# Matrix-memory attention: the weight blocks of a head added on VectorE, and one product with ones per head in place of one per block

## The chip, the cores and the metric

One NeuronCore of one Trainium2 chip runs the whole program. The metric is the device time of one execution in microseconds (us). "Before" is given as the median of several runs; the profile is of one more execution, whose own time stands beside its span. Engines: PE is TensorE (its weight loads are listed as PEld), DVE is VectorE, ACT is ScalarE, POOL is GpSimd, SP issues the transfers of the weights.

## The reference, cut to what matters

The program is two transformer blocks over 512 tokens of width 1024. The change touches one stage of the second block, the matrix-memory (mLSTM) attention with 4 heads of width 128:

```python
def mlstm_chunkwise(q, k, v, i_pre, f_pre):      # computed chunk by chunk in the reference
    ...
    w_intra = jnp.exp(d_log - m_t[..., None])    # decay weights, causal
    s_qk = jnp.einsum('bhctd,bhcsd->bhcts', qc, kc) * w_intra
    num = jnp.einsum('bhcts,bhcse->bhcte', s_qk, vc) + ...
    den = jnp.sum(s_qk, axis=-1) + ...
    h = num / jnp.maximum(jnp.abs(den), jnp.exp(-m_t))[..., None]
...
    hm = mlstm_chunkwise(...)
    hm = rms_norm(hm, ml_norm.reshape(ML_HEADS, ML_HEAD_DIM))
    y_ml = jax.nn.sigmoid(o) * hm.reshape(bsz, s, ML_WIDTH)
```

For every query t, `num` is the decayed scores times the values, and `den` is the sum of the same decayed scores over all keys s up to t. Then the result is normalized and gated. The kernel computes the whole sequence of 512 queries at once, without the chunks: score times exp(difference of gates), masked to keys not after the query.

## The kernel before, in words

The five engines each have a queue in which the instructions stand in the order of the program text; engines wait for each other by semaphores. A signal such as `st_done(n)` means "the semaphore has counted n of these". A wait at the head of a queue holds everything behind it. The whole kernel is a list of stages, and each stage appends one function per engine. The matrix-memory stage is `s_mlstm`; after it comes `s_hyout`, the output projection.

In `s_mlstm` the work of a head `hd` (0 to 3) is cut into four units by blocks of 128 keys, `j` = 0 to 3. Unit `u = 4 * hd + j`. Because the mask is causal, unit j covers only the queries from 128 j on: 512, 384, 256 and 128 columns. Keys lie on the partitions, queries along the columns.

For each unit:

- TensorE, `scores(u)` (L2827): keys times queries into PSUM bank `u % 2`.
- ScalarE, `w(u)` (L2882): the decay weights into `msw`. GpSimd cuts the diagonal block of 128 columns to the causal mask (`affine_select`, L2973).
- VectorE (L2948): `mst` = `msw` times the scores in PSUM. It increments `st_done`.
- TensorE, `sums(u)`: first `mst` times the values into bank 4 + hd % 2 (L2838), then `mst` times a 128x128 matrix of ones into bank 6 + hd % 2 (L2840), both accumulated over the four units. The second gives `den` on all partitions.

For each head: `spread(hd)` (L2817, L2818) lays a row of the gates over all partitions for the weights; `finish(hd)` (L2847, L2848) does the same for the lower bound of the denominator; ScalarE's `magnitude(hd)` (L2887, L2888) squares `den` into `mden` and `num` into `msq`; VectorE's `larger(hd)` (L2927) takes the maximum of `mden` and the bound; TensorE's `squares(hd)` (L2854, L2856) sums squares over the width; ScalarE's `rms(hd)` takes Ln and Exp (L2894, L2897) into `mrb`; VectorE's `gain(hd)` (L2931, L2934) multiplies by it and by the output gate into `mnum`; ScalarE's `high` and VectorE's `low` split the result into `yh` and `yl` (L2901, L2938). `act_high` (L2786) and `dve_low` (L2790) do the same for the other half of the layer, within units 4 and 7.

The order of the queues is written out by hand. TensorE's, for each u: `scores(u + 2)`, which waits for `st_done(u + 1)`, that is for the `mst` product of unit u; then `sums(u)`; at j = 1 `spread(hd + 1)` and `squares(hd - 1)`; at j = 3 `finish(hd)`. VectorE's, for each u: the `mst` product; at j = 0 `larger(hd - 1)`; at j = 1 `low(hd - 2)`; at j = 3 `gain(hd - 1)`. ScalarE's, for each u: `w(u + 2)`; at j = 0 `magnitude(hd - 1)` and `high(hd - 2)`; at j = 2 `rms(hd - 1)`. Of the head 3, `magnitude`, `larger`, `rms` and `gain` come after the loop, and its `squares` (`last_squares`, L2980) stands inside the next stage.

GpSimd's queue goes on behind the last mask cut with splitting the weights of the next stage (`wlo`, L299, L300).

Of the kernel before, what the change touches and what calls it, by code (L numbers as in the profile page):

```python
# [18 lines left out]
ALU = mybir.AluOpType  # L19
AX = mybir.AxisListType.X  # L20

P = 128
# [71 lines left out]
def program(nc, d, out):  # L94
    with ExitStack() as ctx:
# [133 lines left out]
        mgt = at("mgt", X + 8192, [P, T])  # L229
        mnum = at("mnum", B + 82064, [P, 2, T])  # L230
        mden = at("mden", B + 86160, [P, T])

        prj = at("prj", B, [P, DT, T])

# [2558 lines left out]
        def s_mlstm(before):  # L2793
# [4 lines left out]
            def part(buffer, j, first=0, last=T):  # L2798
# [3 lines left out]
             ss_done, ln_done, rb_done, t_done, p_done, h_done, l_done) = local(  # L2802
                "st", s=16, m=4, w=16, st=16, cut=16, pv=16, nm=4, abs=4, mx=4, sq=4, ss=4, ln=4,
                rb=4, t=4, p=4, h=4, l=4)

            def pe(pe):

                def spread(hd):

                    if hd >= 2:  # L2810
                        pe.wait_ge(*mx_done(hd - 1))
                    if hd == 0:
                        pe.wait_ge(*scaled(20))
                        pe.wait_ge(*row_high(3))
                        pe.wait_ge(*row_low(2))
                    pick = selr[:, hd * P:(hd + 1) * P]
                    pe.matmul(PS3[:, 2 + hd % 2, :], pick, rowsr[:, 3, :], start=True, stop=False, skip_group_check=True)  # L2817
                    pe.matmul(PS3[:, 2 + hd % 2, :], pick, rowsr[:, 4, :], start=False, stop=True,  # L2818
                              skip_group_check=True).then_inc(m_done.s, 1)

                def scores(u):
                    hd, j = units[u]
                    if u >= 2:
                        pe.wait_ge(*st_done(u - 1))
                    elif u == 0:
                        pe.wait_ge(*key_scaled(1))
                    pe.matmul(PS3[:, u % 2, j * P:T], qkc[:, 4 + hd, j * P:(j + 1) * P], qkc[:, hd, j * P:T],  # L2827
                              start=True, stop=True, skip_group_check=True).then_inc(s_done.s, 1)

                def sums(u):  # L2830
                    hd, j = units[u]
                    pe.wait_ge(*st_done(u + 1))
                    if hd == 0:
                        pe.wait_ge(*v_kept(max(2, j + 1)))
                    if hd >= 2 and j == 0:
                        pe.wait_ge(*t_done(hd - 1))
                        pe.wait_ge(*ln_done(hd - 1))
                    pe.matmul(PS3[:, 4 + hd % 2, j * P:T], vml[:, j, hd * P:(hd + 1) * P], part(mst, j, j * P),  # L2838
                              start=j == 0, stop=j == 3, skip_group_check=True)
                    pe.matmul(PS3[:, 6 + hd % 2, j * P:T], c_("ones"), part(mst, j, j * P),  # L2840
                              start=j == 0, stop=j == 3, skip_group_check=True).then_inc(pv_done.s, 1)

                def finish(hd):

                    pe.wait_ge(*w_done(4 * hd + 4))
                    pick = selr[:, hd * P:(hd + 1) * P]
                    pe.matmul(PS3[:, 2 + hd % 2, :], pick, rowsr[:, 0, :], start=True, stop=False, skip_group_check=True)  # L2847
                    pe.matmul(PS3[:, 2 + hd % 2, :], pick, rowsr[:, 2, :], start=False, stop=True,  # L2848
                              skip_group_check=True).then_inc(nm_done.s, 1)

                def squares(hd):
                    pe.wait_ge(*sq_done(hd + 1))
                    pe.wait_ge(*mx_done(hd + 1))
                    pe.matmul(PS3[:, 6 + hd % 2, :], c_("ones"), msq[:, :], start=True, stop=False,  # L2854
                              skip_group_check=True)
                    pe.matmul(PS3[:, 6 + hd % 2, :], c_("ones"), mden[:, :], start=False, stop=True,  # L2856
                              skip_group_check=True).then_inc(ss_done.s, 1)
                spread(0)
                scores(0)
                scores(1)  # L2860
                pe_values(pe, 3)
                for u in range(16):
                    hd, j = units[u]
                    if u + 2 < 16:
                        scores(u + 2)
                    sums(u)
                    if j == 1 and hd < 3:
                        spread(hd + 1)
                    if j == 1 and hd >= 1:
                        squares(hd - 1)  # L2870
                    if j == 3:
                        finish(hd)

            def act(act):
                act.preload_act_table_set("natural_log_exp_and_others")

                def w(u):
                    hd, j = units[u]
                    act.wait_ge(*m_done(hd + 1))
                    if u >= 4:  # L2880
                        act.wait_ge(*st_done(u - 3))
                    act.activation(part(msw, j, j * P), PS3[:, 2 + hd % 2, j * P:T], ACT.Exp,  # L2882
                                   bias=ccol[:, j, hd:hd + 1], scale=-1.0).then_inc(w_done.s, 1)

                def magnitude(hd):
                    act.wait_ge(*pv_done(4 * hd + 4))
                    act.activation(mden[:, :], PS3[:, 6 + hd % 2, :], ACT.Square, scale=EPS ** 0.5).then_inc(abs_done.s, 1)  # L2887
                    act.activation(msq[:, :], PS3[:, 4 + hd % 2, :], ACT.Square).then_inc(sq_done.s, 1)  # L2888

                def rms(hd):  # L2890
                    act.wait_ge(*ss_done(hd + 1))
                    if hd >= 1:
                        act.wait_ge(*t_done(hd))
                    act.activation(mrb[:, :], PS3[:, 6 + hd % 2, :], ACT.Ln, bias=epsc[:, 4:5],  # L2894
                                   scale=1.0 / P).then_inc(ln_done.s, 1)
                    act.wait_ge(*ln_done(hd + 1))
                    act.activation(mrb[:, :], mrb[:, :], ACT.Exp, scale=-0.5).then_inc(rb_done.s, 1)  # L2897

                def high(hd):
                    act.wait_ge(*p_done(hd + 1))  # L2900
                    act.activation(yh[:, 4 + hd, :], mnum[:, hd % 2, :], ACT.Copy).then_inc(h_done.s, 1)  # L2901
                w(0)
                w(1)
                act_last_split(act)
                for u in range(16):
                    hd, j = units[u]
                    if u + 2 < 16:
                        w(u + 2)
                    if hd >= 1 and j == 0:
                        magnitude(hd - 1)  # L2910
                    if hd >= 2 and j == 0:
                        high(hd - 2)
                    if hd >= 1 and j == 2:
                        rms(hd - 1)
                    if u in rg_steps["act"]:
                        rg_steps["act"][u](act)
                magnitude(3)
                high(2)
                rms(3)
                high(3)  # L2920

            def dve(dve):
# [13 lines left out]
                def low(hd):  # L2936
                    dve.wait_ge(*h_done(hd + 1))
                    dve.tensor_tensor(yl[:, 4 + hd, :], mnum[:, hd % 2, :], yh[:, 4 + hd, :].bitcast(F32),  # L2938
                                      ALU.subtract).then_inc(l_done.s, 1)
                for u in range(16):  # L2940
                    hd, j = units[u]
                    if u == 0:
                        dve.wait_ge(*gated(1))
                    dve.wait_ge(*s_done(u + 1))
                    dve.wait_ge(*cut(u + 1))
                    if u >= 4:
                        dve.wait_ge(*pv_done(u - 3))
                    dve.tensor_tensor(part(mst, j, j * P), part(msw, j, j * P), PS3[:, u % 2, j * P:T],  # L2948
                                      ALU.mult).then_inc(st_done.s, 1)
                    if u == 0:  # L2950
                        dve_value(dve, 0)
                        dve_value(dve, 1)
                    elif u < 3:
                        dve_value(dve, u + 1)
                    if u in rg_steps["dve"]:
                        rg_steps["dve"][u](dve)
                    if hd >= 1 and j == 0:
                        larger(hd - 1)
                    if hd >= 2 and j == 1:
                        low(hd - 2)  # L2960
                    if hd >= 1 and j == 3:
                        gain(hd - 1)
# [780 lines left out]
```

## Time and profile before

| | |
|---|---|
| median of 3 runs | 2518.85 us (2516.84 to 2520.12) |
| the profiled execution, its own time | 2519.44 us |
| its span, first to last instruction | 2517.7 us |
| TensorE busy | 2488.9 us, 99% |
| VectorE busy | 1421.9 us, 56% |
| ScalarE busy | 1045.1 us, 42% |
| GpSimd busy | 972.7 us, 39% |
| mean granted TensorE clock | 0.997 |
| the matrix-memory stage on TensorE | about 1355.4 to 1398.9 us |

Busy time of an engine says how much it could be in the way, not that it is. The chain that ended last is followed back from the last instruction, at each step to what released it; its pieces add up to the span, so what stands in it is what the time is made of. In the chain a matrix product is shown by the time that it adds, in the time line by its own length, which overlaps the next one by some 0.16 us. A product of plain float32 operands is listed as two records; "x2" in a row is one product.

### The profile page before, as it was taken

The numbers are of one execution on the slowest core, as the hardware profiler recorded it, in microseconds if no ns is written. First come the engines' busy times: TensorE is split into PE (matmuls) and PEld (weight loads), VectorE is DVE, ScalarE is ACT, GpSimd is POOL, SyncE is SP. The second block draws the span as 40 slices with busy tenths as digits, with TensorE's granted clock in tenths as the row PEclk, the third lists the DMA queues.
The fourth block names the chain that finished last, engine by engine and source line by source line (L and its number), as shares of the span: only waits on it lengthen the run. The fifth ranks groups of instructions, "written<-read, shape, count | busy, mean of one in ns | idle before, by whom it ended". The sixth has DMA issues, their size and how long they took to land.

```text
span 2517.7 us, 37538 instructions
## 1 busy us (share of the span) xinstructions
PE 2488.9 (99%) x13732; PEld 2104.4 (84%) x13732; DVE 1421.9 (56%) x1894; ACT 1045.1 (42%) x1551; POOL 972.7 (39%) x721
## 2 busy tenths in 40 slices
PE   9999999999999989999999999999999999999999
PEld 8999999957777789988777788888887778888887
DVE  6988114376436688841595655553355855666213
ACT  5556224374343455542564332222244643222222
POOL 3001553303234400045353555555453045555443
PEclk9999999999999999999999999999999999999999
DMA  4333332202112222333321223232332122222322
GB/s 161 101 105 95 109 104 99 78 1 68 59 59 94 96 87 100 100 115 96 109 93 51 85 99 99 92 100 92 100 126 80 55 86 99 100 92 100 105 97 84
DMA packets 72187, 230.96 MB, mean 92 GB/s; under 512 B 9297, under 2 KB 9553, under 8 KB 72082
## 3 DMA queue, kind: packets, MB, share of 16 engines
q1 hardware_dynamic: 64128, 216.27, 26.2%
q10 hardware_dynamic: 7954, 13.26, 1.7%
q8 instruction: 69, 1.13, 0.2%
q14 instruction: 36, 0.29, 0.0%
HBM read 220.58 MB, written 5.24 MB: 90 GB/s over the span
## 4 chain that ended last, share of the span: by engine, by line
PE 63%; DVE 1%; ACT 0%; issue 0%; DVEq 0%; ACTq 0%
PE PS L305 17%; PE PS L307 17%; PE PS L306 17%; PE PS L811 2%; PE PS L812 2%; PE PS L813 2%; PE PS L3374 1%; PE PS L3391 1%; PE PS L3355 1%; PE PS L2827 0%; PE PS L2840 0%; PE PS L2838 0%; PE PS L3159 0%; PE PS L3362 0%; PE PS L2445 0%; PE PS L2444 0%
## 5 line engine op out<-in xcount | busy, mean ns | idle before, releaser
L299 POOL TENSOR_TENSOR wlo<-wraw,whi 128x512 fp32r<-128x512 f32 (+2 forms) x350 | 458.5, 1310 | 1481.3 <-ACT whi L291 1481.1
L305 PE MATMUL PS<-xh,whi 128*128 128x512 f32 (+1 forms) x1640 | 608.7, 371 | 3.9 <-POOL wlo L300 1.6
L307 PE MATMUL PS<-xh,wlo 128*128 128x512 f32 (+1 forms) x1640 | 601.7, 367 | 0.0
L306 PE MATMUL PS<-xl,whi 128*128 128x512 f32 (+1 forms) x1640 | 601.4, 367 | 0.0
L291 ACT ACTIVATE whi<-wraw 128x1024 fp32r<-128x1024 f32 (+2 forms) x350 | 350.2, 1001 | 594.0 <-PE PS L307 579.4
L300 POOL TENSOR_TENSOR wlo<-wraw,whi 128x512 fp32r<-128x512 f32 (+2 forms) x350 | 522.5, 1493 | 0.0
L305 PEld LDWEIGHTS PS<-xh,whi 128*128 128x128 f32 x1640 | 307.4, 187 | 59.6 <-POOL wlo L300 2.5
L307 PEld LDWEIGHTS PS<-xh,wlo 128*128 128x128 f32 x1640 | 307.5, 187 | 51.3
L306 PEld LDWEIGHTS PS<-xl,whi 128*128 128x128 f32 x1640 | 307.5, 187 | 51.1 <-issue 1.4
L305 PE MATMUL PS<-hid2h,whi 128*128 128x512 f32 x560 | 218.4, 390 | 0.0
L306 PE MATMUL PS<-hid2l,whi 128*128 128x512 f32 x560 | 217.9, 389 | 0.0
L307 PE MATMUL PS<-hid2h,wlo 128*128 128x512 f32 x560 | 217.9, 389 | 0.0
L1441 DVE TENSOR_TENSOR h<-PS,h 128x512 f32<-128x512 f32 x24 | 16.6, 690 | 204.9 <-PE PS L307 204.9
L1257 DVE TENSOR_TENSOR gp<-PS,rb_up 128x1024 f32<-128x1024 f32 x24 | 29.4, 1224 | 174.2 <-PE PS L307 174.2
L1544 DVE TENSOR_SCALAR f<-PS 128x528 f32<-128x528 f32 (+1 forms) x16 | 11.2, 699 | 203.9 <-ACT sq L1528 193.4
L305 PEld LDWEIGHTS PS<-hid2h,whi 128*128 128x128 f32 x560 | 105.1, 188 | 22.9 <-DVE h L1441 0.8
L306 PEld LDWEIGHTS PS<-hid2l,whi 128*128 128x128 f32 x560 | 105.1, 188 | 21.9 <-issue 0.2
L307 PEld LDWEIGHTS PS<-hid2h,wlo 128*128 128x128 f32 x560 | 105.1, 188 | 21.7
L493 ACT ACTIVATE xh<-h,vec 128x512 fp32r<-128x512 f32 (+1 forms) x64 | 45.9, 726 | 156.9 <-DVE h L1441 107.0
L1267 DVE SCALAR_TENSOR_TENSOR gc<-gp,vec,gc 128x512 f32<-128x512 f32 x96 | 111.0, 1213 | 0.0
L305 PE MATMUL PS<-hid1h,whi 128*128 128x264 f32 x352 | 100.3, 285 | 0.0
L306 PE MATMUL PS<-hid1l,whi 128*128 128x264 f32 x352 | 100.3, 285 | 0.0
(546 smaller groups left out, 5170.2 us busy)
## 6 DMA issues: line engine op xcount, KB each, us to landing
wraw<-w_up_dram SPq DMA_DIRECT2D x96, 512.0 KB, 3.2
wraw<-w_dn_dram SPq DMA_DIRECT2D x48, 512.0 KB, 3.2
wraw<-w_f1gu_dram SPq DMA_DIRECT2D x44, 512.0 KB, 3.2
wraw<-w_f2gu_dram SPq DMA_DIRECT2D x44, 512.0 KB, 3.2
wraw<-w_hyin_dram SPq DMA_DIRECT2D x24, 512.0 KB, 3.3
wraw<-w_win_dram SPq DMA_DIRECT2D x18, 512.0 KB, 3.3
wraw<-w_gate_dram SPq DMA_DIRECT2D x16, 512.0 KB, 3.2
wraw<-w_pg_dram SPq DMA_DIRECT2D x16, 512.0 KB, 3.3
```

The costliest lines, as they stand in the source:

```text
L291: act.activation(whi[:, s, 0:size], wraw[:, s, 0:size], ACT.Copy).then_inc(hi_done.s, 1)
L299: pool.tensor_tensor(wlo[:, s, 0:half], wraw[:, s, 0:half], whi[:, s, 0:half].bitcast(F32), ALU.subtract)
L300: pool.tensor_tensor(wlo[:, s, half:size], wraw[:, s, half:size], whi[:, s, half:size].bitcast(F32), ALU.subtract).then_inc(lo_done.s, 1)
L305: pe.matmul(out_, whi[:, s, a:b], xhi, start=start, stop=False, skip_group_check=True)
L306: pe.matmul(out_, whi[:, s, a:b], xlo, start=False, stop=False, skip_group_check=True)
L307: return pe.matmul(out_, wlo[:, s, a:b], xhi, start=False, stop=stop, skip_group_check=True)
L493: act.activation(dh[:, t, 0:n], h[:, t, 0:n], ACT.Copy, scale=v_(gain, t)).then_inc(high.s, 1)
L811: pe.matmul(o, oph[:, jj, a], high[:, kt, :], start=start and kt == 0, stop=False, skip_group_check=True)
L812: pe.matmul(o, oph[:, jj, a], low[:, kt, :], start=False, stop=False, skip_group_check=True)
L813: ins = pe.matmul(o, opl[:, jj, a], high[:, kt, :], start=False, stop=kt == 3, skip_group_check=True)
L1257: dve.tensor_tensor(gp[:, :, 2:T + 2], bank(0, 2), spread(rb_up, 1), ALU.mult).then_inc(g_read.s, 1)
L1267: ins = dve.scalar_tensor_tensor(gc[:, m, :], gp[:, m, tap:T + tap], vec[:, bass.ds(2 * j + (cw + FF2T * tap + m), 1)], gc[:, m, :], ALU.m ...
```

## The change

`sums(u)` no longer issues the product with ones. In its place VectorE adds the `mst` blocks of a head into a tile `macc` of 512 columns (two tiles, for even and odd heads): behind the `mst` product of each unit comes `add(u)`, at j = 0 a copy of the first 128 columns, and at j = 1, 2, 3 an add of the 384, 256 and 128 columns from 128 j on; at j = 1 the earlier part is read from the unit 0 block itself. TensorE issues one product of ones with the whole `macc` per head, `over_keys(hd)`, 512 columns: for heads 0 to 2 behind the sums of unit 4 hd + 4, for head 3 behind `finish(3)`, at the end of the stage. `magnitude(hd)` waits for it by a new signal.

```diff
+        macc = [at("macc0", B + 95568, [P, T]), at("macc1", B + 88208, [P, T])]
...
+            added, summed_over = local("su", add=16, over=4)
...
                     pe.matmul(PS3[:, 4 + hd % 2, j * P:T], vml[:, j, hd * P:(hd + 1) * P], part(mst, j, j * P),
-                              start=j == 0, stop=j == 3, skip_group_check=True)
-                    pe.matmul(PS3[:, 6 + hd % 2, j * P:T], c_("ones"), part(mst, j, j * P),
                               start=j == 0, stop=j == 3, skip_group_check=True).then_inc(pv_done.s, 1)
+
+                def over_keys(hd):
+                    pe.wait_ge(*added(4 * hd + 4))
+                    pe.matmul(PS3[:, 6 + hd % 2, :], c_("ones"), macc[hd % 2][:, :], start=True, stop=True,
+                              skip_group_check=True).then_inc(summed_over.s, 1)
...
                     if u + 2 < 16:
                         scores(u + 2)
                     sums(u)
+                    if j == 0 and hd >= 1:
+                        over_keys(hd - 1)
                     if j == 1 and hd < 3:
                         spread(hd + 1)
                     if j == 1 and hd >= 1:
                         squares(hd - 1)
                     if j == 3:
                         finish(hd)
+                over_keys(3)
...
                 def magnitude(hd):
                     act.wait_ge(*pv_done(4 * hd + 4))
+                    act.wait_ge(*summed_over(hd + 1))
                     act.activation(mden[:, :], PS3[:, 6 + hd % 2, :], ACT.Square, scale=EPS ** 0.5).then_inc(abs_done.s, 1)
...
+                def add(u):
+                    hd, j = units[u]
+                    over = macc[hd % 2]
+                    dve.wait_ge(*st_done(u + 1))
+                    if j == 0:
+                        if hd >= 2:
+                            dve.wait_ge(*summed_over(hd - 1))
+                        dve.tensor_copy(over[:, 0:P], part(mst, 0, 0, P)).then_inc(added.s, 1)
+                    else:
+                        dve.wait_ge(*added(u))
+                        so_far = part(mst, 0, P) if j == 1 else over[:, j * P:T]
+                        dve.tensor_tensor(over[:, j * P:T], so_far, part(mst, j, j * P), ALU.add).then_inc(added.s, 1)
...
                     dve.tensor_tensor(part(mst, j, j * P), part(msw, j, j * P), PS3[:, u % 2, j * P:T],
                                       ALU.mult).then_inc(st_done.s, 1)
+                    add(u)
```

## Rows read from the trace of the kernel before

**Rows 1.** The page: busy time of the engines, and the chain that ended last.
```profile
PE 2488.9 (99%) x13732; PEld 2104.4 (84%) x13732; DVE 1421.9 (56%) x1894; ACT 1045.1 (42%) x1551; POOL 972.7 (39%) x721
...
PE 63%; DVE 1%; ACT 0%; issue 0%; DVEq 0%; ACTq 0%
```

**Rows 2.** The chain, in order of time: start, length, engine and line.
```profile
1372.79 0.86 PE PS L2840 x2
...
1374.52 0.65 PE PS L2840 x2
...
1375.82 1.05 PE PS L2854 x2
1376.88 0.86 PE PS L2856 x2
...
1379.02 0.43 PE PS L2840 x2
...
1380.32 0.24 PE PS L2840 x2
1380.56 0.68 DVE mst L2948
1381.28 0.70 PE PS L2827 x2
...
1385.64 0.23 PE PS L2818
```

**Rows 3.** The time line of VectorE: start, length, line, tiles, idle before and releaser.
```profile
1374.67 2.29 DVE L2790 TENSOR_TENSOR yl<-grg,yh 128x2048 fp32r<-128x2048 f32 x1
1379.15 0.75 DVE L2931 SCALAR_TENSOR_TENSOR mgt<-PS,vec,mrb 128x512 f32<-128x512 f32 x1 [2.19 <-ACT mrb L2897]
...
1381.28 0.69 DVE L2927 TENSOR_TENSOR mden<-mden,PS 128x512 f32<-128x512 f32 x1
1381.89 0.55 DVE L2948 TENSOR_TENSOR mst<-msw,PS 128x384 f32<-128x384 f32 x1
1382.35 0.68 DVE L2938 TENSOR_TENSOR yl<-mnum,yh 128x512 fp32r<-128x512 f32 x1
```

**Rows 4.** The time line of ScalarE, the same columns.
```profile
1371.66 1.92 ACT L2786 ACTIVATE yh<-grg 128x2048 fp32r<-128x2048 f32 x1
...
1377.77 0.69 ACT L2894 ACTIVATE mrb<-PS,epsc 128x512 f32<-128x512 f32 x1 [1.23 <-PE PS L2856]
1378.49 0.63 ACT L2897 ACTIVATE mrb<-mrb 128x512 f32<-128x512 f32 x1
...
1380.58 0.60 ACT L2887 ACTIVATE mden<-PS 128x512 f32<-128x512 f32 x1 [0.63 <-PE PS L2840]
```

**Rows 5.** The list of TensorE's waits: us in total, times, longest us.
```profile
PEld PS L1822 <- DVE spf L1877: 9.4, 12, 1.7
...
PEld PS L2827 <- DVE mst L2948: 1.3, 3, 0.5
```

**Rows 6.** The time line of TensorE, the same columns as rows 3.
```profile
1380.82 0.39 PE L2848 MATMUL PS<-rowsr,selr 4*128 4x512 f32 x1
1381.28 0.70 PE L2827 MATMUL PS<-qkc 128*128 128x256 f32 x2
```

**Rows 7.** Groups by shape, 1355.38 to 1398.88: count, then busy us, mean ns.
```profile
L2948 DVE TENSOR_TENSOR mst<-msw,PS 128x128 f32<-128x128 f32 x4 | 1.1, 284 | 2.6 <-PE PS L2827 2.6
```

**Rows 8.** Time lines of VectorE and GpSimd at the start of the next stage.
```profile
1400.63 1.00 DVE L2938 TENSOR_TENSOR yl<-mnum,yh 128x512 fp32r<-128x512 f32 x1
```
```profile
1399.35 1.74 POOL L300 TENSOR_TENSOR wlo<-wraw,whi 128x512 fp32r<-128x512 f32 x1
```

**Rows 9.** Three windows: us, busy PE PEld DVE ACT POOL, granted clock, DMA share, GB/s.
```profile
903.00:907.00 4.00, 0.00 (x0) 0.00 (x0) 2.39 (x3) 3.99 (x5) 0.00 (x0) 0.61 0.00 0
907.00:911.00 4.00, 3.98 (x19) 3.98 (x20) 4.00 (x5) 1.43 (x2) 0.00 (x0) 0.54 0.44 136
500.00:510.00 10.00, 8.92 (x54) 6.05 (x53) 7.17 (x9) 8.43 (x11) 0.00 (x0) 1.00 0.00 0
```

## The prediction

> **What bounds the kernel now.** I read the page first. [rows 1] TensorE is busy for 99% of the span, no other engine for more than 56%, and the chain that ended last runs through TensorE almost alone. So 1 us taken off TensorE's queue is 1 us of time, as long as TensorE does not start to wait for something; and every us that it is made to wait counts in full. Next I read the stage that the change touches, by the chain of waits in order of time over one head (hd = 1) [rows 2]. The reader is to see a solid row of TensorE pieces with one other link: VectorE's `mst` product at 1380.56. Then the same head on VectorE and ScalarE [rows 3, 4]: both have holes, so their work costs nothing unless it stands between two TensorE pieces. Last the list of waits [rows 5]: in these four heads TensorE's score product waits for VectorE 3 times, 1.3 us in all. All times in us.
>
> I call the units 0 to 15 u, with hd = u // 4 and j = u % 4; "sums" is the product with the values (L2838) and "ones" the product with ones behind it (L2840).
>
> **What TensorE no longer does.** Each product shows as two records, and the chain gives the pair. Ones cost 0.86 at j = 0, 0.65 at j = 1, 0.43 at j = 2 and 0.24 at j = 3, where I count 0.22 (a quarter of the 0.86) and leave the rest to the step to `finish` [rows 2]. That is 2.16 a head, 4 x 2.16 = 8.64 in all.
>
> **What it does instead.** One full-width product a head, the shape of the 0.86: 4 x 0.86 = 3.44. For hd = 0 to 2 it stands behind sums of the next head's j = 0, among products of its own kind. The fourth comes behind `finish(3)`, where the operand type changes: after such a change the same shape took 1.05 and not 0.86 [rows 2], so 0.19 more. TensorE's own work: -8.64 + 3.44 + 0.19 = **-5.0**.
>
> **What it has to wait for now.** This decides. Before, the last ones of head 0 came at the end of unit 3, and ScalarE's `magnitude` (the squares into `mden` and `msq`) ran while TensorE did `finish` and the scores and sums of unit 4. Look at hd = 1, 2: `mden` starts at 1380.58 [rows 4], as TensorE still has `finish` and a score product to do, and VectorE takes `larger` at 1381.28 without idling [rows 3]. After the change the sum over keys of head hd - 1 is issued behind the sums of unit 4hd. What comes next in TensorE's queue are the scores of unit 4hd + 3. They wait for `st_done` of unit 4hd + 1, that product stands in VectorE's queue behind `larger(hd - 1)`, `larger` waits for `mden`, and `mden` waits for the new product. A closed loop with no other work in TensorE's queue to cover it. Its price, link by link: TensorE's end to ScalarE's start 0.04 (1376.88 + 0.86 is 1377.74, `mrb` starts 1377.77) [rows 2, 4]; `mden` 0.60 [rows 4]; ScalarE to VectorE 0.03 (1378.49 + 0.63 is 1379.12, `mgt` starts 1379.15) [rows 3, 4]; from the start of `larger` to the next product 0.61 (1381.28 to 1381.89), and that product 0.55 [rows 3]; VectorE to TensorE 0.05 (1380.56 + 0.68 is 1381.24, start 1381.28); and the first product after a wait takes 0.70 in the chain where that width otherwise takes 0.43 (1379.02), so 0.27 [rows 2]. Sum 2.15. It happens at hd = 1, 2 and 3: 3 x 2.15 = **6.45**.
>
> The second wait is there already. At j = 1 TensorE issues `squares(hd - 1)`; then ScalarE's Ln and Exp (1377.77, 1378.49), VectorE's `gain` (from 1379.15), then the product of unit 4hd + 4 (1380.56), which the next scores wait for [rows 2 to 4]. From the end of `squares` (1377.74) that chain takes 3.5, fixed. TensorE's own work in that stretch was only just shorter: free at 1380.82 + 0.23 = 1381.05 and started at 1381.28, a wait of 0.23 [rows 6] (the 0.23 added is what such a product takes in the chain [rows 2]). The change takes the ones of j = 2 and j = 3 out of this stretch, 0.65; they turn into 0.65 more of wait. This holds for the stretches of hd = 1 and 2 (before units 8 and 12): 2 x 0.65 = **1.30**. Behind head 3 no such wait follows, the next stage goes on at once.
>
> **VectorE's new work.** Sixteen steps: a copy of 128 columns, then adds of 384, 256 and 128. The adds are not in the trace; the nearest are `mst` products of the same width, 0.55 for 384 [rows 3] and 0.28 for 128 [rows 7], 0.4 between them for 256. For the copy I take 0.28, between nothing and the 0.55 of 384 columns. About 1.5 a head, 6 in all, each with its wait on the product before it (some 0.04). None stands in the first loop: add(4hd) is ahead of `larger` while VectorE waits anyway, and add(4hd + 1) comes behind the product that TensorE wants. If that cover were gone, one copy would cost 0.3 a head, 0.9. In the second chain the add of unit 7 pushes `dve_low`, 2.29 long [rows 3], against `gain(0)`. Here `act_high` (1.92 [rows 4]) and unit 7's weights follow `magnitude` on ScalarE. Counted from the end of the new product: the two squares and `act_high` end at about 3.1, unit 7's weights, their mask cut and its product at 4.2, the add at 4.5, `dve_low` at 6.8; `gain(0)` is due at 2.15 + 3.5 for the scores, sums, `spread` and `squares` + 1.4 for Ln and Exp = 7.1. Some 0.3 is left, so nothing. In head 0 the adds push the value evictions by 0.3 to 0.5 each; by my count of that queue the tightest product, unit 3's, still ends 0.4 before the scores of unit 5 want it: nothing.
>
> **Contention.** The adds and the copy read SBUF alone, two tensors in the adds, and from the last mask cut on GpSimd splits the next stage's weights without a pause. With GpSimd quiet `yl` took 0.68 and beside the splits 1.00, and a split 1.74 [rows 3, 8]. In head 3 the adds of units 14 and 15 fall there. Counted from the end of head 2's sum: product of unit 15 done about 4.7, its add 5.1 unhindered; the last sum over keys is due at 6.1. So 1.0 of cover, against one split half of up to 1.74 in the way: 0 to 0.8. I take 0, as the add's own slowing by the `yl` rows is 0.3. The Trainium skill, "SBUF — State Buffer", section "SBUF: two separate sides", speaks against this part of the change: VectorE with two SBUF inputs and GpSimd share a port pair under an exclusive lock, and the loser waits for the whole instruction. The rows agree that both slow down, not that either waits a full one; by that rule the last add would end at about 6.0 and the sum stay as it is.
>
> **Sum.** -5.0 + 6.45 + 1.30 = **+2.7**. Checked by place: head 0 gives 2.16; head 1 and head 2 each lose 2.15 - 0.65 = 1.50; head 3 with the last sum loses 2.15 - 0.65 - 0.65 + 1.05 = 1.90. -2.16 + 3.00 + 1.90 = 2.74. On the profiled execution that is 2519.44 + 2.7 = 2522.2. The profiled execution is 0.6 above the median of the runs, so the forecast for the median is 2518.85 + 2.7 = **2521.6**, which is 0.11% and inside the 0.2% (5.0 us) that a measurement can tell from no change.
>
> **Rivals.**
> (a) The product count decides, and the waits do not appear: -5.0, 2513.8. For it speaks that TensorE is the bound all along; against it the order of the queues, written out by hand, in which VectorE cannot pass `larger`. Half of the loop hidden (1.1 each) would give -5.0 + 3.2 + 1.3 = -0.5. Chance of the full gain 0.05.
> (b) Slower by over 0.2%: TensorE's clock falls in the new gaps. One gap of some 8 us brought the granted clock to 0.61 and then 0.54 on average over the next 4 us (most of them at the lower of its two levels, 1.2 GHz) [rows 9], which costs 4 x 0.46 = 1.8 of work. If each of the three waits of 2.15 did so: 2.7 + 5.5 = 8.2, 2527. It decides from two such falls on. Against it: TensorE was idle 1.08 of 10 us in the stage at 500, in gaps of up to 1.7, and the clock there stayed at 1.00 [rows 5, 9]. Chance 0.05. The Trainium skill, "TensorE: Matmul & The Clock Gate", section "HAM oscillation — how this bites in real kernels", says that gaps between bursts of products can throttle the engine again and again; that no gap here comes near the 8 us one is why I leave it at that chance.
> (c) The loops are longer than their links: contention in head 3 (0.8), the copy in each loop (0.9), the cover at `gain(0)` gone (0.5). Together 4.9, 2523.7, still inside the band; anything more is outside. Chance 0.17, a third of it above 5.0.
> (d) The change does nothing on TensorE because the ones are hidden already: excluded, the chain holds them [rows 2].
>
> **How the numbers follow.** Forecast 0.73 (its own range +0.5 to +4.5: 2519.3 to 2523.3), (a) 0.05, (b) 0.05, (c) 0.17. The range 2517.0 to 2525.5 takes in the half-hidden loop at 2518.3 and (c), and a us or so of spread of the medians; it leaves out (a) and (b). Faster by over 0.2% 0.06, within 0.2% 0.80, slower 0.14.
>
> **What would show it.** TensorE's new waits in the list: its score product waiting for `mst` in total 3 x 1.9 + 2 x 0.9, near 7.5 instead of 1.3. In the time line a TensorE gap behind each of the first three sums over keys, filled by `mden`, `larger` and `mst` in this order. The start of `finish(3)`'s following stage 2.7 later than before. Four ones products of 512 columns, 3.4 in all. The forecast is wrong if the gap behind the sums is not there (then the queue order was misread), if the granted clock is under 1.00 in the stage, or if an add stands last before a TensorE start.

## The result, and the profile after

The changed kernel takes 2526.96 us (median of 9 runs, 2524.51 to 2528.25), the kernel before 2518.94 (9 runs, 2516.84 to 2520.12): 8.0 us more, ratio 1.0032, 95% interval 1.0023 to 1.0041. The forecast was 2521.6, range 2517.0 to 2525.5. The measured time lies outside it, at the 2527 of rival (b), the fall of TensorE's clock (chance 0.05).

The page of the changed kernel, answering to [rows 1]: TensorE is busy 1.6 us longer than before, although it has 24 records less.

```profile
PE 2490.5 (99%) x13708; PEld 2101.5 (83%) x13708; DVE 1428.2 (57%) x1910; ACT 1046.3 (41%) x1551; POOL 976.3 (39%) x721
```

The chain of waits of the changed kernel over the same head, answering to [rows 2] (start, length, engine and line; the lines have moved: L2829 is the score product, L2840 the sums, L2845 the new sum over keys, L2859 and L2861 `squares`):

```profile
1368.51 0.86 PE PS L2840 x2
1369.37 0.87 PE PS L2845 x2
...
1370.32 0.61 ACT mden L2896
...
1371.63 0.56 DVE mst L2969
...
1372.23 0.49 PE PS L2829 x2
1372.72 0.65 PE PS L2840 x2
...
1374.37 2.00 PE PS L2859 x2
1376.37 1.71 PE PS L2861 x2
1378.08 1.71 PE PS L2829 x2
1379.79 0.76 PE PS L2840 x2
1380.54 0.65 PE PS L2829 x2
```

Two things are to be seen. Between 1370.24 and 1372.23 there is no TensorE piece: the predicted loop of `mden`, `larger` and `mst`, in this order (`larger` stands in the time line below, at 1371.02). And from 1373.4 on TensorE's own pieces are too long: the two products of `squares` take 2.00 and 1.71, where they took 1.05 and 0.86 [rows 2], the score product 1.71 in place of 0.86. The score product at 1380.54 is back at 0.65. None of them waited for another engine; the granted clock says why. Windows of the changed kernel (us, busy PE PEld DVE ACT POOL, granted clock, DMA share, GB/s):

```profile
1366.00:1370.00 4.00, 4.00 (x14) 2.09 (x12) 0.96 (x3) 0.43 (x2) 0.59 (x2) 1.00 0.01 2
1370.00:1374.00 4.00, 2.00 (x7) 0.87 (x6) 2.55 (x6) 3.14 (x4) 0.29 (x1) 0.94 0.00 0
1374.00:1378.00 4.00, 4.00 (x6) 1.64 (x6) 2.70 (x3) 0.69 (x1) 1.73 (x1) 0.50 0.00 0
1378.00:1382.00 4.00, 4.00 (x11) 2.09 (x10) 2.27 (x4) 2.15 (x4) 1.05 (x2) 0.71 0.00 0
...
1390.00:1394.00 4.00, 4.00 (x6) 1.62 (x5) 0.00 (x0) 1.23 (x3) 0.07 (x1) 0.50 0.00 0
...
1400.00:1404.00 4.00, 3.33 (x6) 1.85 (x7) 3.90 (x8) 0.62 (x2) 3.31 (x3) 0.60 0.02 4
```

The clock drops to 0.50, the lower level of 1.2 GHz, behind the first gap and again behind the second, and it falls behind the third too, for a shorter time (0.60 on average over the last window). "Busy 4.00 of 4.00" in the windows at 0.50 is TensorE at half speed, which is why its busy time did not fall. The Trainium skill, "TensorE: Matmul & The Clock Gate", section "HAM oscillation — how this bites in real kernels", tells of waits between bursts of products that bring the clock down again and again. The trace agrees in that, with three falls in one stage; but the waits of the section's example are longer than the 2.0 here, and how short a gap can be is taken from the runs alone.

The time lines of VectorE and TensorE, answering to [rows 3, 6]:

```profile
1371.02 0.69 DVE L2936 TENSOR_TENSOR mden<-mden,PS 128x512 f32<-128x512 f32 x1 [4.03 <-ACT mden L2896]
1371.63 0.55 DVE L2969 TENSOR_TENSOR mst<-msw,PS 128x384 f32<-128x384 f32 x1
1372.21 0.56 DVE L2960 TENSOR_TENSOR macc<-mst 128x384 f32<-128x384 f32 x1
```
```profile
1369.20 1.02 PE L2845 MATMUL PS<-macc,con 128*128 128x512 f32 x2
1372.23 0.49 PE L2829 MATMUL PS<-qkc 128*128 128x128 f32 x2 [2.00 <-DVE mst L2969]
...
1386.42 0.49 PE L2829 MATMUL PS<-qkc 128*128 128x128 f32 x2 [2.00 <-DVE mst L2969]
...
1400.67 0.70 PE L2829 MATMUL PS<-qkc 128*128 128x128 f32 x2 [2.00 <-DVE mst L2969]
```

And its list of waits, answering to [rows 5]: 9.7 in place of 1.3, where near 7.5 was forecast.

```profile
PEld PS L2829 <- DVE mst L2969: 9.7, 6, 2.8
```

This row counts the time without a weight load, and the forecast was worked out from TensorE's time without a product, so the two can't be compared. Of the products themselves, three wait for `mst`, 2.00 each, as the time line shows. The longer wait of the second chain does not show in this kernel: the slowed products fill its stretch.

**Where the 8 us are.** I measure the stage from the start of `spread(0)` to the first product of the next stage that reads `yl`. Before: 1355.38 to 1399.21, 43.8. After: 1354.11 to 1407.64, 53.5, so 9.7 more. The stage began 1.3 earlier in this execution than in that of before, which the change does not touch: 1.2 of it is a fall of the clock at 757 us that the execution of before had and this one had not (more on it under E8 to E10). Spans differ by 8.7.

### The profile page after: what moved, and what is told of

Same layout as the page of the kernel before. It is cut to its first block, busy times and chain, and to the rows that moved or that the text cites. A ratio compares the mean times of both kernels' runs of the same rounds, so it can differ in the third digit from the quotient of the medians.

```text
span 2526.4 us, 37524 instructions
## 1 busy us (share of the span) xinstructions
PE 2490.5 (99%) x13708; PEld 2101.5 (83%) x13708; DVE 1428.2 (57%) x1910; ACT 1046.3 (41%) x1551; POOL 976.3 (39%) x721
## 3 DMA queue, kind: packets, MB, share of 16 engines
q8 instruction: 69, 1.13, 0.2%
## 4 chain that ended last, share of the span: by engine, by line
PE 94%; DVE 3%; ACT 2%; issue 1%; DMA 0%; SPq 0%; ACTq 0%; DVEq 0%
PE PS L306 23%; PE PS L308 23%; PE PS L307 23%; PE PS L812 5%; PE PS L814 5%; PE PS L813 5%; PE PS L3396 1%; PE PS L2179 1%; PE PS L1823 1%; PE PS L3413 1%; PE PS L2829 0%; PE PS L3377 0%; PE PS L2205 0%; PE PS L1807 0%; PE PS L2840 0%
```

## The experiments

Two theories. **C**: the waits cost what I summed (+2.7), and the rest is the clock, which falls in the gaps. **L**: the loops and the adds take longer than the links that I summed. Each kernel was timed beside the kernel before, whose median was 2519.10 (E1 to E4), 2519.40 (E5 to E8) and 2519.49 (E9 to E11). "Stage" is measured in the profiled execution as above, against 43.8.

### E1: the gaps filled with four products

```diff
                     if j == 0 and hd >= 1:
                         over_keys(hd - 1)
+                        fill(pe, 6 + hd % 2, 4)
```

`fill` issues products of ones, 128 x 256, whose results nobody reads.

> The changed kernel, with four products of ones (128 x 256, 0.43 us each) put into TensorE's queue behind the sum over keys of heads 0, 1 and 2, into the PSUM bank of the current head that nobody reads there. Their results are overwritten. The wait for VectorE stays as it is, TensorE is only busy in most of it. Theory C (the waits cost what I summed, +2.7, and the other 5.3 is TensorE's clock, which falls after each idle gap of some 2 us): granted clock 1.00 in the whole stage, idle before the scores under 0.4 each, time 2521.6, that is before + 2.7. Theory L (the loops and the adds are longer than their links, and the clock is a side show): the 1.7 us of filler run in time that was idle, so the time stays at 2527.

Measured: 2522.72 (2519.44 to 2523.25), ratio 1.0013 [1.0004, 1.0022]; stage 46.8, +2.9. The time line of its TensorE, and two windows:

```profile
1368.17 1.02 PE L2845 MATMUL PS<-macc,con 128*128 128x512 f32 x2
1369.03 1.89 PE L314 MATMUL PS<-con 128*128 128x256 f32 x8
1371.19 0.49 PE L2829 MATMUL PS<-qkc 128*128 128x128 f32 x2 [0.28 <-DVE mst L2970]
...
1372.92 1.13 PE L2859 MATMUL PS<-msq,con 128*128 128x512 f32 x2
...
1377.33 0.39 PE L2853 MATMUL PS<-rowsr,selr 4*128 4x512 f32 x1
1378.45 0.70 PE L2829 MATMUL PS<-qkc 128*128 128x256 f32 x2 [0.73 <-DVE mst L2970]
```
```profile
1370.00:1374.00 4.00, 3.72 (x14) 1.88 (x13) 3.55 (x8) 3.11 (x4) 0.51 (x2) 1.00 0.00 0
1374.00:1378.00 4.00, 3.72 (x13) 1.89 (x11) 3.33 (x4) 2.15 (x4) 2.90 (x3) 1.00 0.00 0
```

The scores start 3.02 behind the start of the sum over keys, against 3.03 in the changed kernel: the wait is as long as it was. But the clock stays at 1.00, `squares` takes its old 1.13, and 4.2 us of the median are gone although TensorE does 5.2 us more of useless work. Theory C holds, theory L (2527) falls. What is left is the price of the order of the queues, and it can be taken apart in this profile. TensorE's own work: the last sum over keys costs 0.87, not 1.05 (it hides the change of type that was paid at the stage's end before), so -8.64 + 3 x 0.86 + 0.87 = -5.2. The loop: 3.02 - 0.86 = 2.16, and 0.11 for the first product behind it (0.33 to the next start instead of 0.22), 3 x 2.27 = 6.8. The second chain: TensorE is free at 1377.33 + 0.23 = 1377.56 and starts at 1378.45, a wait of 0.89 in place of 0.23, twice 0.66 = 1.3. Sum +2.9, the +2.9 of the stage; the forecast had 2.7. The median is 3.6 above that of before, 0.7 more than the stage explains; its interval, +1.0 to +5.5, takes in both.

### E2 and E11: shorter gaps

The same with 2 and with 1 in place of the 4 products, which leaves gaps of 1.1 and 1.57 us (the time line's idle time in front of the scores).

> The same with two products of ones in each gap instead of four: 0.86 us of filler, idle gaps of some 1.1 us left. Theory C in the form 'short gaps do no harm' (the stage at 500 us has gaps of up to 1.7 and keeps its clock): clock 1.00, 2521.6 as with four. If the gap of 1.1 is already enough for a fall in this stage: as the changed kernel, 2527. Theory L: 2527.

> The changed kernel with one filler product (0.43 us) in each of the three gaps: idle gaps of some 1.6 us. With two products (gaps of 1.1) 3 of 11 runs stood at 2525.6 to 2526.8 with a clock of 0.995 to 0.996, the others at 2519.6 to 2522.5; with four none. If the idle time decides how often the clock falls: more runs in the upper group than 3 of 11, median 2523 to 2526. If it does not: as with two.

Measured: E2 2522.31, 1.0015 [1.0006, 1.0024]; E11 2525.99, 1.0023 [1.0013, 1.0033]. All runs, lowest first, with those of the mean granted clock of 0.996 or less behind the bar:

```
E1, four products  2519.4 2520.3 2520.9 2521.5 2522.6 2522.7 2522.8 2522.9 2523.0 2523.0 2523.3 |
E2, two products   2519.6 2520.0 2520.6 2520.9 2521.6 2522.3 2522.5 2522.5 | 2525.6 2526.1 2526.8
E11, one product   2519.8 2521.2 | 2524.6 2525.9 2526.0 2526.1 2526.1 2526.2 2526.3
```

The stage of E11's profiled execution, one of the two without a fall, is 46.7 long, as E1's. So the same kernel has two times, some 4 us apart, with nothing between 2523.3 and 2524.6, and the upper one goes with the lower clock. Shorter gaps make it rarer: none of 11 runs, 3 of 11, 7 of 9. I had expected all or nothing of the two-product kernel; it is a share of the runs. That the upper time is a fall in this stage is read from times and mean clocks: both profiled executions, E2's and E11's, have a clock of 1.00 throughout the stage. Nor do these runs tell whether the length of the gap decides or the work that fills it, since both change together.

### E3: the wait alone, on the kernel before

```diff
                 def magnitude(hd):
-                    act.wait_ge(*pv_done(4 * hd + 4))
+                    act.wait_ge(*pv_done(min(4 * hd + 5, 16)))
```

> The kernel before with the wait of the change alone: the product with ones stays, one per block, nothing is added on VectorE, but ScalarE's magnitude(hd) waits for the ones of the next head's first block, which is where the change puts its product. Nothing is taken off TensorE. Without a fall of the clock: 3 x 2.15 = 6.45, 2525.4. Theory C: the same gaps of about 2 us, three falls, 5 to 7 more: 2531, and a granted clock near 0.5 to 0.6 for some 3 us behind each gap. Theory L (the adds and the new product are what cost): at most 6.45, since they are not there.

Measured: 2529.46, ratio 1.0040 [1.0026, 1.0053], 5 runs; stage 53.7, +9.9. Three gaps of 1.94 us, and in this execution one fall, behind the second, where three and a time of 2531 were expected. The time line of its TensorE (L2854 is the first product of `squares`):

```profile
1375.72 0.49 PE L2827 MATMUL PS<-qkc 128*128 128x128 f32 x2 [1.94 <-DVE mst L2948]
...
1378.09 1.13 PE L2854 MATMUL PS<-msq,con 128*128 128x512 f32 x2
...
1387.98 0.49 PE L2827 MATMUL PS<-qkc 128*128 128x128 f32 x2 [1.94 <-DVE mst L2948]
...
1392.00 2.08 PE L2854 MATMUL PS<-msq,con 128*128 128x512 f32 x2
```

The wait alone, without an add and with every product with ones in place, makes the kernel 10.4 us slower, more than the change does. The loop is 1375.72 - 1372.76 - 0.86 = 2.10 here (the ones before it start at 1372.76), with the 0.11 of the first product three times 6.6 of the stage's 9.9; the one fall is the other 3.3.

### E4: `larger` behind the product that TensorE wants

```diff
-                    if hd >= 1 and j == 0:
+                    if hd >= 1 and j == 1:
                         larger(hd - 1)
```

> The changed kernel with one step moved: on VectorE larger(hd - 1) stands behind the mst product of j = 1 and its add, not ahead of it, so that TensorE's next scores do not wait for it. Theory C and my sum: no gap, no fall; -5.0 for TensorE's own work and +1.3 for the second chain: before - 3.7, 2515.2, clock 1.00 in the stage. Theory L (the adds and the longer chains themselves): no faster than before, 2519 or more. If squares now waits for the maximum, up to 0.3 a head more.

Measured: 2519.80, ratio 1.0002 [0.9993, 1.0012]; stage 44.9, +1.0. My sum missed by 4.4. The time line of its TensorE:

```profile
1371.72 0.50 PE L2819 MATMUL PS<-rowsr,selr 4*128 4x512 f32 x1 [0.67 <-DVE mden L2936]
...
1376.79 0.39 PE L2853 MATMUL PS<-rowsr,selr 4*128 4x512 f32 x1
1378.74 0.70 PE L2829 MATMUL PS<-qkc 128*128 128x256 f32 x2 [1.55 <-DVE mst L2969]
1379.27 1.19 PE L2840 MATMUL PS<-mst,vml 128*128 128x512 f32 x2
1380.25 1.91 PE L2845 MATMUL PS<-macc,con 128*128 128x512 f32 x2
```

I had read past a wait: `spread(hd + 1)` overwrites the bank that `larger(hd - 1)` reads and waits for it, so the loop's wait moved a few products on and only shrank. The second chain was also longer than 0.9. TensorE reached `squares` earlier, ScalarE's `act_high` did not end earlier, and so unit 7's product, its add and `dve_low` still held VectorE when `gain(0)` was due at 1375.8; it started at 1376.62. That is the thin cover which the prediction named, gone: a wait of 1.7 (1377.02 to 1378.74, listed as 1.55 idle), and behind it the clock fell here too: 1.91 for a product that otherwise shows 1.02, and a granted clock of 0.50 from 1380 to 1382. That is 7.2 us taken off the changed kernel, but not one us won.

### E5 and E6: the sum over keys behind the head's own sums

```diff
                     sums(u)
-                    if j == 0 and hd >= 1:
-                        over_keys(hd - 1)
...
                     if j == 3:
+                        if hd < 3:
+                            over_keys(hd)
                         finish(hd)
                 over_keys(3)
```

E6 also moves `gain(hd - 1)` on VectorE behind the `mst` product and the copy of the next head's first unit.

> The changed kernel with one step moved on TensorE: for heads 0, 1 and 2 the sum over keys stands straight behind the head's own last sums, ahead of finish, and not behind the sums of the next head's first unit. ScalarE's and VectorE's links then run under finish, a score product and sums, as before the change. Theory C: no gap of 2 us, no fall; own work -5.0, the second chain +1.3, and at most 0.1 a head of wait for the last add: before - 3.4, 2515.7, clock 1.00 in the stage. Theory that some other cost of the adds remains: no faster than 2519.

> As the last one, and on VectorE gain(hd - 1) stands behind the mst product of the next head's first unit and not ahead of it, which takes the second chain (squares, Ln, Exp, gain) off the way to the next scores. Theory C with my sum: the 1.3 goes and so do the two waits of 0.23 of the kernel before: -5.0 + 0.3 - 0.46, before - 5.1, 2514.0. If larger, now behind gain, comes too late for the next scores, up to 0.5 a head of it is given back.

Measured: E5 2513.41 (2512.04 to 2514.87), ratio 0.9979 [0.9970, 0.9988]; E6 2514.37, ratio 0.9982 [0.9973, 0.9991]. Both stages are 38.7 long, -5.1. The time line of E5's TensorE around the second chain:

```profile
1373.82 1.02 PE L2861 MATMUL PS<-mden,con 128*128 128x512 f32 x2
...
1376.84 1.02 PE L2845 MATMUL PS<-macc,con 128*128 128x512 f32 x2
...
1378.13 0.38 PE L2853 MATMUL PS<-rowsr,selr 4*128 4x512 f32 x1
1378.45 0.70 PE L2829 MATMUL PS<-qkc 128*128 128x256 f32 x2
```

One step in TensorE's queue turns 8.0 us lost into 6.0 won: the same adds, the same number of products. I had expected -3.4. Most of the missing 1.7 of the stage is the second chain: the sum over keys, 0.86, now stands in the stretch between `squares` and the scores of the next head but one, and fills it better than the 0.65 of ones did that it replaces. Not even the old wait of 0.23 is left. That is also why E6, which was to take this wait away, has nothing to take: same stage, and a median within the other's interval.

### E7: the adds alone

VectorE's copies and adds in the kernel before, read by nobody; the products with ones stay.

> The kernel before with VectorE's copies and adds alone: the products with ones stay, one per block, and nobody reads the sums that VectorE makes. Theory C: the 16 steps, some 6 us of VectorE, lie in its idle time: within 0.5 of before, 2519.1. Theory L (the adds are part of the cost): 2521 or more, with score products waiting longer for mst.

Measured: 2519.56, ratio 1.0002 [0.9993, 1.0011]; stage 43.8, as before. In the order of the kernel before the adds cost nothing that shows.

### E8 to E10: which gaps

The filler of E1 left out of one or two gaps. E8 leaves the third gap idle (`if hd < 3`), E9 the first (`if hd > 1`), E10 the first two (`if hd > 2`).

> The changed kernel with the four filler products in the gaps of heads 0 and 1, and the third gap, behind the sum over keys of head 2, left idle. Behind the third gap stand 3.0 us of TensorE work in the stage and then the next stage, of which the changed kernel's profile shows 1.7 lost. Theory C: the time with four fillers in all gaps (before + 3.6) and, if the one gap that is left is enough for a fall in every run, 1.7 to 3 more: 2524.4 to 2526; if it falls in some runs only, between 2522.7 and 2525 and a wider spread of runs. Theory L: no change from the filler kernel, 2522.7.

> The changed kernel with the four filler products in the gaps of heads 1 and 2, so that the first gap, behind the sum over keys of head 0, is the only idle one. The kernel with the third gap left never fell (highest run 2522.6). Theory A (one gap of 2.0 us does not bring the clock down, it takes several in a row): 2521.5 to 2523, all runs within 3 us of each other. Theory B (each gap can, by chance or by what stands around it, and the third is only the mildest): part of the runs near 2525, 2 to 3.5 us above the rest, with a mean clock of 0.996 or less.

> The same with the filler in the gap of head 2 alone, so that the first two gaps are idle. Theory A: falls behind the second gap, 2524 to 2526 in the median. Theory B: two chances to fall, median between the kernel with one gap left and the changed kernel's 2527, with two or three separate groups of runs.

Measured: E8 2521.99 (2521.11 to 2522.59), 1.0011 [1.0002, 1.0020]; E9 2524.71 (2522.33 to 2526.39), 1.0021 [1.0011, 1.0030]; E10 2525.97 (2524.10 to 2527.67), 1.0027 [1.0018, 1.0036]. The time line of E9's TensorE, with its one gap, and that of E10's behind its second:

```profile
1373.82 0.49 PE L2829 MATMUL PS<-qkc 128*128 128x128 f32 x2 [2.00 <-DVE mst L2971]
...
1375.72 2.08 PE L2859 MATMUL PS<-msq,con 128*128 128x512 f32 x2
1377.59 1.57 PE L2861 MATMUL PS<-mden,con 128*128 128x512 f32 x2
```
```profile
1385.52 0.49 PE L2829 MATMUL PS<-qkc 128*128 128x128 f32 x2 [2.00 <-DVE mst L2971]
...
1387.55 2.08 PE L2859 MATMUL PS<-msq,con 128*128 128x512 f32 x2
```

One gap is enough: the fall in E9's profile makes its stage 1.6 longer than E1's (48.4 against 46.8), its median is 2 above E1's, and 10 of its 11 runs lie above E1's highest. That is theory B of these runs, that each gap can bring the clock down, though not in each execution. E9 decides it; E10's 2526.0 was expected by both theories. The medians rise with the number of gaps, one 2524.7, two 2526.0, three 2527.0, though the intervals overlap. The mean clock of a run, which I wanted to go by, is too coarse a sign: E9's profiled execution has its fall at a mean of 0.997, E4's at 0.998.

The exception is the third gap. E8, which was expected at 2522.7 or more, has no run above E1's highest, and its profile no fall. So the third gap alone, just as long, brought no fall that shows, although the changed kernel's profile has one behind it (0.60 above). Behind the third gap come full products and no `spread`, and in front of it stands the same work as before the others. Why it is milder stays open. Nor does the same gap act the same in each execution: the first gap left the clock alone in the profiles of E3 and E10 and brought it down in those of E9 and the changed kernel.

**A gap that no kernel here changes.** The clearest case stands at 757 us, far ahead of the stage. TensorE waits 1.47 there in every kernel, the one before too. The time line and one window of before, then the same of the changed kernel:

```profile
756.62 0.50 PE L305 MATMUL PS<-ysbh,whi 128*128 128x512 f32 x1 [1.47 <-DVEq L321]
756.00:760.00 4.00, 3.38 (x9) 2.66 (x10) 0.51 (x1) 3.40 (x5) 0.51 (x1) 0.64 0.42 131
```
```profile
756.60 0.50 PE L306 MATMUL PS<-ysbh,whi 128*128 128x512 f32 x1 [1.48 <-DVEq L322]
756.00:760.00 4.00, 3.40 (x15) 2.83 (x16) 0.49 (x1) 3.42 (x5) 0.48 (x1) 1.00 0.38 131
```

The clock fell behind it in 7 of the 13 profiled executions (before, E2, E3, E5, E6, E7, E9) and stayed at 1.00 in the other 6. From this product to the end of TensorE's work before the gap of 7.6 at 899 it takes 142.6 to 142.8 with the fall and 141.6 without, in the same work: 1.2 for one fall. So here, too, the same gap brings the clock down in about half of the executions.

## Why the prediction was wrong, point by point

- **TensorE is the bound, TensorE's own work falls by 5.0**: right, 5.2 in E1.
- **The closed loop, 3 x 2.15 = 6.45**: right in place and order; 3 x 2.27 = 6.8. Both hand-overs, to ScalarE and to VectorE, took 0.10 (1369.20 + 1.02 to 1370.32, 1370.92 to 1371.02) instead of the 0.04 and 0.03 that I had read elsewhere. (The 0.27 of the prediction and the 0.11 here are the same cost of the first product: 0.16 of it, by which one product overlaps the next, is counted with the product there and with the loop here.)
- **The second chain, +1.30**: right where the clock is held up, 1.3 in E1; in the changed kernel the slowed products cover it.
- **VectorE's adds cost nothing**: right. They took 0.56, 0.43 and 0.29, the copy 0.23 (forecast 0.55, 0.4, 0.28, 0.28), and E7 shows no cost. The contention was put too low: beside GpSimd's splits the last two adds took 1.04 each in E1 instead of 0.42 and 0.29, 0.6 and 0.75 more where I had taken 0.3. The last add ended 6.1 behind the end of head 2's sum, as the prediction gave it for a wait of a full instruction (6.0), and not at 5.1; some 0.2 of the 1.0 of cover was left (1398.47 to 1398.65), so it cost nothing.
- **Sum +2.7**: right for the queues, +2.9 in the stage with the clock held up; the own work came out 0.2 lower and the loops 0.35 higher, which partly cancel. The changed kernel is not that kernel.
- **The failed step: TensorE's clock put at nothing, rival (b) at a chance of 0.05.** The prediction had two rows for it: a gap of some 8 us that brought the clock down, and a stage with gaps of up to 1.7 that kept it [rows 5, 9]. Gaps of 2.15 lie between, and I put them with the harmless ones because they were nearer in length. That is an argument from one stage, and the stage was misread. The 1.7 of [rows 5] is a wait of the weight loads; the products themselves were never idle for more than 1.27 there, and for 0.86 in the window of [rows 9]:

```profile
527.55 0.19 PEld L1822 LDWEIGHTS PS<-sph,cr 128*128 128x128 f32 x1 [1.72 <-DVE spf L1877]
527.56 0.33 PE L1822 MATMUL PS<-sph,cr 128*128 128x128 f32 x1 [1.27 <-DVE spf L1877]
```

And the same trace held the counterexample, the gap of 1.47 at 757 us with a granted clock of 0.64 behind it. What the runs showed in place of the 0.05: behind idle gaps of 2.0 the clock fell three times out of three in the changed kernel's profile, and with the gaps filled not at all (E1). The price of the rival was nearly right, 5.5 for three falls; the median of the changed kernel is 4.2 above that of E1, the profiled execution's stage 6.8. That the median lies at the rival's 2527 is partly chance: the profiled execution, with all three falls, took 2528.1.

- **The range** stopped at 2525.5 and so left out rival (b), whose price stood in the text, though nothing in the trace bounded its chance. The chances do not add up either: slower by over 0.2% is 0.05 of (b) and a third of the 0.17 of (c), 0.11, and 0.14 was given.
- **What would show it**: the gap behind the sums was there, in the order given. The granted clock under 1.00 in the stage was named as a sign of a wrong forecast, and it is the one that came.

## What to carry to other kernels

Work taken off the bounding engine pays only if what it is replaced by does not come between two of its instructions; follow each new signal round the queues until it comes back to the engine that sends it, and if it does, put the product where work already queued covers the way round. Price a gap on TensorE as its length and a chance of lower clock behind it: here 2.2 us of gap and some 1.2 to 3.3 us more when the clock fell. Before you call a gap harmless, look in the trace of before for TensorE's own idle gaps of that length, not those of its weight loads, and read the granted clock behind each; and look in more than one execution. If the order cannot be changed, products that nobody reads, put into the gap, give the clock part back: 4.2 us here, with the wait itself left as it was.

## What the runs showed of the hardware that I had not expected

- TensorE's granted clock fell to 0.50 behind idle gaps of 2.0 us, and also behind one of 1.55 (E4) and of 1.47 (at 757 us); on the evidence of run times and mean clock, with no trace of it, also behind gaps of 1.57 (7 of 9 runs) and of 1.1 (3 of 11).
- It is a matter of chance from run to run: the gap of 1.47 at 757 us, which no kernel changes, brought the clock down in 7 of 13 profiled executions; E11 stands at 2519.8 to 2521.2 and at 2524.6 to 2526.3; and of three equal gaps in one execution of E3 one brought a fall.
- One fall cost 1.2 (at 757 us), 1.6 (E9), 2.5 (E10) and 3.3 (E3). It costs less where a wait follows that the slowed products can fill: in E10 the wait of 0.9 of the second chain is gone behind the fall.
- A slowed product counts as busy: the changed kernel has less work and 1.6 us more of TensorE busy time. Only the granted clock in fine windows tells the two apart; the mean of the run moves by 0.002 (0.997 to 0.995).
